# A hybrid decoder step: order of requests and updates around the state stage, and row weights made during routing

## The reference, cut to what matters

```python
# attention (prompt: causal softmax over 256 keys; samples: over 2048 cached keys and their own)
pr = softmax(scores * SCALE);  o_attn = (pr @ v) @ w_o_attn
# state-space branch, prompt, two chunks of 128 tokens, 16 heads in 2 groups
seg = a_cum[:, :, :, None] - a_cum[:, :, None, :]
y_diag = einsum((C B^T) * exp(seg), xdt)              # inside a chunk
chunk_states = einsum(B, exp(a_cum[-1] - a_cum), xdt)
h_final = chunk_decay * h + chunk_states              # h after chunk one is used by chunk two
y_off = einsum(C, h_prev, exp(a_cum))
# state-space branch, samples
h = h * exp(a_t) + outer(x_t * dt_t, b_t);  y = h . c_t      # h is [16, 64, 128] per sample
# gate, norm and output projection, then the mix of the branches
y = rms_norm((y + d_skip * x) * silu(z), g_ssd);  o_ssd = y @ w_o_ssd
merged = sigmoid(gate_a) * o_attn + sigmoid(gate_b) * o_ssd;  x = x + g1 * rms_norm(merged @ w_out)
# experts: sigmoid scores, 4 of 8 groups, 6 of 64 experts, weights normalised to 2.5
w = take(scores, e_idx);  w = w / sum(w) * 2.5
routed = sum_e (silu(t @ w_gate_e) * (t @ w_up_e) * w[:, e]) @ w_down_e
y = x + g2 * rms_norm(routed + shared)
```

## Time and profile before

| what | us |
|---|---|
| median of 3 runs (947.97 to 951.63) | 948.81 |
| the profiled execution | 949.16 |
| its span, first to last instruction | 947.1 |
| PE busy in it | 897.6 (95%) |
| DVE, ACT, POOL busy | 329.3, 201.5, 154.1 |
| bytes read and written, MB | 326.65 and 15.81 |

### The profile page before, as it was taken

One profiled execution on the slowest core, in us unless ns is written; L12 is line 12 of the kernel. 1 busy time (PEld: TensorE's weight loads), 2 busy tenths in 40 slices (PEclk: granted clock), 3 DMA queues, 4 the chain that ended last, 5 costly groups with the idle time before them and its releaser, 6 DMA issues.

```text
span 947.1 us, 18258 instructions
## 1 busy us (share of the span) xinstructions
PE 897.6 (95%) x7475; PEld 556.5 (59%) x7475; DVE 329.3 (35%) x826; ACT 201.5 (21%) x506; POOL 154.1 (16%) x185
## 2 busy tenths in 40 slices
PE   5999999998899799898899999999999999999996
PEld 3888888876565477656744445544454545455442
DVE  2325570056344588346223221221122222221224
ACT  2000110326132398033111111110111111111102
POOL 0000000041565000000212212121212212122110
PEclk9999999999999999999999999999999999999998
DMA  9966757645699819997899999999999999999992
GB/s 367 406 227 232 303 211 291 242 146 202 221 349 348 348 56 316 409 421 295 310 413 400 425 415 426 415 422 419 424 416 424 418 422 419 423 418 423 418 402 107
DMA packets 61237, 325.47 MB, mean 344 GB/s; under 512 B 16321, under 2 KB 25394, under 8 KB 40610
## 3 DMA queue, kind: packets, MB, share of 16 engines
q1 hardware_dynamic: 47250, 305.54, 80.3%
q0 software_dynamic: 12176, 18.56, 5.8%
q10 hardware_dynamic: 1728, 0.18, 0.1%
HBM read 326.65 MB, written 15.81 MB: 362 GB/s over the span
## 4 chain that ended last, share of the span: by engine, by line
PE 45%; DMA 5%; DVE 1%; issue 0%; POOL 0%; ACT 0%
PE bank L2354 22%; PE bank L2294 12%; PE bank L2305 6%; DMA slot_b<-in_w_e 4%; PE bank L2266 3%; DMA xg<-tok_rows,tab_g 1%; PE bank L2388 1%; PE bank L2340 1%; DVE slot_b L2685 0%; DVE slot_b L2693 0%; POOL weight_tab L2214 0%; PE bank L2324 0%; PE bank L2332 0%; ACT slot_b L2498 0%; DVE wgt L2538 0%
## 5 line engine op out<-in xcount | busy, mean ns | idle before, releaser
L420 PE MATMUL bank<-h,ring 128*128 128x264 f32 x608 | 138.4, 388 | 0.5 <-PE bank L420 0.3
L420 PEld LDWEIGHTS bank<-h,ring 128*128 128x128 f32 x608 | 114.6, 190 | 21.9 <-issue 2.8
L2481 ACT ACTIVATE sge<-bank 64x256 f32<-64x256 f32 x64 | 24.1, 377 | 390.6 <-PE bank L2354 390.6
L2584 DVE TENSOR_TENSOR hh<-sge,bank 64x256 f32<-64x256 f32 x64 | 27.1, 423 | 219.0 <-ACT sge L2481 215.5
L2354 PE MATMUL bank<-done_out,xt 128*64 128x256 f32 x832 | 95.5, 382 | 0.0
L2354 PE MATMUL bank<-ring,xt 128*64 128x256 f32 x800 | 91.8, 382 | 0.3 <-ACT xt L2472 0.3
L1668 POOL DMA_INDIRECT xg<-tok_rows,tab_g x32 | 32.0, 1002 | 332.3 <-PE bank L2266 310.6
L2524 DVE COPY sq<-bank 128x512 f32<-128x512 f32 x64 | 44.3, 692 | 104.3 <-PE bank L2294 92.3
L2294 PE MATMUL bank<-ring,ht 128*32 128x512 f32 x320 | 76.4, 598 | 0.0
L2354 PEld LDWEIGHTS bank<-done_out,xt 128*64 128x64 f32 x832 | 57.9, 137 | 27.6
L2305 PE MATMUL bank<-sq,wmat 64*128 64x512 f32 x256 | 72.0, 640 | 0.0
(11 more groups left out here) (486 smaller groups left out, 1245.8 us busy)
## 6 DMA issues: line engine op xcount, KB each, us to landing
done_out<-in_w_e SPq DMA_DIRECT2D x26, 2048.0 KB
ring<-in_w_units SPq DMA_DIRECT2D x25, 2048.0 KB, 10.6
ring<-in_w_e SPq DMA_DIRECT2D x24, 2048.0 KB
slot_b<-in_w_e SPq DMA_DIRECT2D x13, 2048.0 KB
ring<-in_w_e SPq DMA_DIRECT2D x19, 1024.0 KB
slot_b<-in_w_e SPq DMA_DIRECT2D x10, 1024.0 KB
done_out<-in_w_e SPq DMA_DIRECT2D x10, 1024.0 KB
row_of<-in_w_e SPq DMA_DIRECT2D x10, 1024.0 KB
```

The source lines that it names most:

```text
L420: mm = pe.matmul(bank[:, t % NB, 0:T], w[:, j, k, :], h[:, k, :], start=(k == 0), stop=(k == KD - 1))
L2481: act.activation(sg[e % 2][:, :], bank[0:LB, 4, 0:FE], ACT.Silu).then_inc(sg_ready, 1)
L2584: dve.tensor_tensor(hh[e % 2][:, :], sg[e % 2][:, :], bank[LB:2 * LB, 4, 0:FE], ALU.mult).then_inc(hh_ready, 1)
```

## The change: what it does

Seven edits. (1) In prompt attention ACT makes one dummy exponential before `off_part(0)`; PE waits for `max_ready1` 1 ahead of the products of L769 and for 2 only ahead of the transposes behind them; DVE runs `normalise(0)` ahead of the `val` copy. (2) SP no longer requests unit U_OA before `ac`; the request of L929 now brings both U_OA and U_OS, behind `ac` and the states of samples 6 and 7. (3) `h_ready6` also counts the copy of h1, so that `prompt_out(g)` and `states(1)` wait for h1 of their group alone. `final_state(1)` runs behind the samples' part, and `take_out(0)` runs in it, behind its h1 copy. (4) PE runs `prompt_norm(1)` before `attn_part(5)`. (5) The last states are updated in another order: 0 and 1 before `mix(0)`, 2 and 3 behind it, 4 and 5 behind `mix(1)` and `mix(2)`, 6 and 7 inside `mix(3)` between its two products. (6) DVE makes the row weights in the routing block, between its two `hs` products, and POOL stores them there; in the experts' block POOL starts with `gather(2)`, then waits for these stores, gathers the first weights, and issues `gather(3)` behind them. (7) ACT issues two of the four y_s stores.

```diff
@@ prompt attention, ACT, PE, DVE
+                            act.activation(sm[:, 0, 0:1], eps, ACT.Exp)
                             off_part(0)
...
-                            pe.wait_ge(max_ready1, 2)
+                            pe.wait_ge(max_ready1, 1)
...
                             mm.then_inc(lat_done, 1)
+                            pe.wait_ge(max_ready1, 2)
...
+                            normalise(0)
                             dve.wait_ge(v_done, 1)
                             dve.tensor_copy(val[:, :, :], bank[:, 6:8, :]).then_inc(side_took, 1)
-                            normalise(0)
@@ sample attention, SP
-                            sp.wait_ge(weighed, 7)
-                            load_units(sp, U_OA + 1)
@@ state stage, SP and PE
-                        sp.wait_ge(h_ready6, 2)
+                        sp.wait_ge(h_ready6, 4)
...
                             if g:
-                                pe.wait_ge(h_ready6, 1)
+                                pe.wait_ge(h_ready6, 2)
...
-                            pe.wait_ge(h_ready6, g + 1)
+                            pe.wait_ge(h_ready6, 2 * g + 1)
...
                             pe.wait_ge(squares_ready, 5 + g)
-                            pe.wait_ge(h_ready6, 2)
+                            pe.wait_ge(h_ready6, 4)
...
                         attn_part(4)
+                        prompt_norm(1)
                         attn_part(5)
-                        prompt_norm(1)
@@ state stage, DVE
-                            link(dve.tensor_copy(h1[:, hs, :], got[0]))
+                            dve.tensor_copy(h1[:, hs, :], got[0]).then_inc(h_ready6, 1)
+                            dve.wait_ge(h_ready6, 2 * g + 1)
+                            if g:
+                                take_out(0)
...
                         weigh_out(1)
-                        final_state(1)
...
-                        take_out(0)
+                        final_state(1)
...
-                        def mix(d):
+                        def mix(d, between=()):
...
+                            for b in between:
+                                update_state(b)
...
-                        for b in range(3):
+                        for b in range(2):
                             update_state(b)
                         mix(0)
-                        update_state(3)
+                        for b in (2, 3):
+                            update_state(b)
                         for d in range(1, KD):
-                            mix(d)
-                            if d + 3 < TS:
+                            mix(d, (TS - 2, TS - 1) if d == 3 else ())
+                            if d < 3:
                                 update_state(d + 3)
@@ routing block, POOL and DVE; weights() itself is moved here
+                        pool.wait_ge(wgt_ready, 1)
+                        for a, n, lo in ((0, P, 0), (2, P, P), (1, TS, TP)):
+                            pool.dma_start(weight_tab[...], wgt[0:n, a, :]).then_inc(tab_stored, 16)
...
                             dve.tensor_tensor(hs[:, i, :], sg[:, i, :], bank[:, 2 + i, 0:T], ALU.mult)
+                            if i == 0:
+                                weights()
@@ experts' block, POOL
-                        pool.wait_ge(wgt_ready, 1)
-                        for a, n, lo in ((0, P, 0), (2, P, P), (1, TS, TP)):
-                            pool.dma_start(weight_tab[...], wgt[0:n, a, :]).then_inc(tab_stored, 16)
                         gather(pool, AHEAD)
-                        gather(pool, AHEAD + 1)
                         pool.wait_ge(tab_stored, 48)
                         gather_weights(0)
                         gather_weights(1)
+                        gather(pool, AHEAD + 1)
@@ tail, SP and ACT
-                        for c in range(4):
+                        for c in (0, 1):
                             store(sp, io["y"][TP:T, c * QD:(c + 1) * QD], y_s[32 * c:32 * c + TS, :])
+                        act.wait_ge(y_done, 3)
+                        for c in (2, 3):
+                            store(act, io["y"][TP:T, c * QD:(c + 1) * QD], y_s[32 * c:32 * c + TS, :])
```

More of the change, by code:

```diff
@@ L1611, in build @@
             tok_i, tok_j = sb("tok_i", [P, NE // 2], I32, stack=moe), sb("tok_j", [P, NE // 2], I32, stack=moe)
+            wgt, need = sb("wgt", [P, NT, NE], stack=moe), sb("need", [P, NT], stack=moe)
+            tab_w, wv = tok_i, tok_j[:, :].bitcast(F32)
             tok_f = sb("tok_f", [P, NE // 2], stack=moe)
@@ L1636, in build @@
             x_in = [sem(f"xg_in{i}", moe) for i in range(AHEAD)]
+            wgt_ready, tab_stored = sem("wgt_ready", moe), sem("tab_stored", moe)
             xt_done, sgu_done, rows_stored = sem("xt_done", moe), sem("sgu_done", moe), sem("rows_stored", moe)
@@ L1756, in _ @@
                             gather(pool, e)
+                        pool.wait_ge(wgt_ready, 1)
+                        for a, n, lo in ((0, P, 0), (2, P, P), (1, TS, TP)):
+                            pool.dma_start(weight_tab[lo * NE:(lo + n) * NE, :].rearrange("(t e) o -> t (e o)", e=NE),
+                                           wgt[0:n, a, :]).then_inc(tab_stored, 16)
                     @block.tensor
@@ L2064, in _, with weights @@
                         link(dve.tensor_tensor(tab_s[:, :], tab_s[:, :], tok_i[0:LB, :], ALU.add))
+                        def weights():
+                            valid = ccol("valid")
+                            place_f = listed_f[:, 0:NE // 2]
+                            dve.memset(wv, 0.0)
+                            link(dve.tensor_scalar(place_f, tok_f[:, :], float(NE), ccol("second"), ALU.mult, ALU.add))
+                            link(dve.scalar_tensor_tensor(tab_w[:, :], ccol("count")[:, 0:NE // 2], 2.0, place_f, ALU.mult, ALU.add))
+                            link(dve.tensor_tensor(wgt[:, :, :], chosen[:, :, :], score[:, :, :], ALU.mult))
+                            link(dve.tensor_reduce(need[:, :], wgt[:, :, :], AX.X, ALU.add))
+                            link(dve.tensor_tensor(need[:, :], need[:, :], valid, ALU.subtract))
+                            link(dve.tensor_scalar(need[:, :], need[:, :], 1.0, None, ALU.add))
+                            link(dve.reciprocal(need[:, :], need[:, :]))
+                            for a in range(NT):
+                                ins = dve.tensor_scalar(wgt[:, a, :], wgt[:, a, :], need[:, a:a + 1], ROUTE, ALU.mult, ALU.mult)
+                            ins.then_inc(wgt_ready, 1)
                         for i in range(2):
@@ L2078, in build @@
                 yo = [flat_sq[:, i * D:(i + 1) * D] for i in range(NYO)]
-                wgt = sb("wgt", [P, NT, NE], stack=ph)
                 e2 = sb("e2", [TS, NE], stack=ph)
-                need = sb("need", [P, NT], stack=ph)
                 cnt = sb("cnt", [1, NE], stack=ph)
@@ L2113, in build @@
                 tok2 = slot_b[:, 5 * (NBLK - NE):6 * (NBLK - NE)]
-                tab_w, wv = tok_i, tok_j[:, :].bitcast(F32)
                 more_f = slot_b[:, 6 * (NBLK - NE):6 * (NBLK - NE) + (ROUNDS - 1) * HB].rearrange("p (r b) -> p r b", b=HB)
@@ L2128, in build @@
                 ht_done, ht_ready, y_ready = sem("ht_done", ph), sem("ht_ready", ph), sem("y_ready", ph)
-                comb_done, wgt_ready, w_ready = sem("comb_done", ph), sem("wgt_ready", ph), sem("w_ready", ph)
+                comb_done, w_ready = sem("comb_done", ph), sem("w_ready", ph)
                 wv_in = [sem(f"wv_in{i}", ph) for i in range(2)]
@@ L2524, in half_out @@
                             dve.tensor_copy(yo[q % NYO][:, h * 512:(h + 1) * 512], bank[:, b, :]).then_inc(y_ready, 1)
-                        def weights():
-                            valid = ccol("valid")
-                            place_f = wmat[0][:, 0:NPAIR]
-                            dve.memset(wv, 0.0)
-                            link(dve.tensor_scalar(place_f, tok_f[:, :], float(NE), ccol("second"), ALU.mult, ALU.add))
-                            link(dve.scalar_tensor_tensor(tab_w[:, :], ccol("count")[:, 0:NPAIR], 2.0, place_f, ALU.mult, ALU.add))
-                            link(dve.tensor_tensor(wgt[:, :, :], chosen[:, :, :], score[:, :, :], ALU.mult))
-                            link(dve.tensor_reduce(need[:, :], wgt[:, :, :], AX.X, ALU.add))
-                            link(dve.tensor_tensor(need[:, :], need[:, :], valid, ALU.subtract))
-                            link(dve.tensor_scalar(need[:, :], need[:, :], 1.0, None, ALU.add))
-                            link(dve.reciprocal(need[:, :], need[:, :]))
-                            for a in range(NT):
-                                ins = dve.tensor_scalar(wgt[:, a, :], wgt[:, a, :], need[:, a:a + 1], ROUTE, ALU.mult, ALU.mult)
-                            ins.then_inc(wgt_ready, 1)
-                            dve.wait_ge(wgt_ready, 1)
                         def weight_of(k):
@@ L2577, in spread_out @@
```

(1 more changed line is left out.)

6 lines of the change are left out of this document (2 added, 4 removed).

## The result

The changed kernel takes 944.38 us in the median of 21 runs (942.18 to 950.22), the kernel before 949.69 us of 21 (946.5 to 953.4). The ratio is 0.9937 with a 95% interval of 0.9925 to 0.995: 0.6% faster, some 6 us (4.7 to 7.1); the medians alone lie 5.3 us apart. The forecast was 943.6 and a gain of 5.2 us. The profiled execution took 944.14 us, its span 942.0 in place of 947.1. Twelve experiments follow, because the sum came out for partly wrong reasons.

A forecast was written before the change was run, and what follows sets the result against it. The stream of experts' weights was taken as the bound, so time saved before it counts. Terms 0.4 + 3.2 + 0.6 + 0.7 + 0.1 + 0.2 = 5.2 us gave 943.6 us from the median 948.81; range 941.3 to 947.8.

The forecast's parts named there:

- What bounds the kernel: Experts' block: the gapless weight stream ends last, so time saved before it counts, PE time saved inside it does not.
- The growing latencies: Experts' block: weight requests needed 19.8 us at 607.75 and 33.4 us at 876.56, read as a growing backlog.
- The prediction's own sign of being wrong: PE's wait for weights near 910 us stays at 1.0 us, not 2.5, while the block gets shorter.
- the gather's term of 0.1: Row weights from routing: PE's 1.56 us wait for gather(2) goes, but only 0.1 us reaches the end; bounds 0 and 1.6.
- The first rival: PE, not the stream, bounds the experts' block; the gather's 1.56 us count in full, 942.1 us; chance 0.15.
- Prompt attention: Table load moved into ACT's idle time, so exponentials start earlier; gain 0.4 us, bounds 0 and 0.9.
- the larger gain: Prompt attention: a drain of about 1.38 us behind the table load would add up to 1.38 us; not counted.
- The state stage with w_out: State stage to the first w_out matmul: that matmul at 392.6, 4.5 us earlier than 397.08.
- the queue's order and h1: State stage: ac ahead of U_OA and h1 counted by itself start the second halves 3.2 us earlier; bounds 2.2 and 4.3.
- the updates: Last states: one fewer update ahead of mix(0) gives 0.6 us; earlier last store and w_out give 0.7 more.
- What I called 0.7 "more": Behind the state stage: w_out lands at about 390, gaining 0.7 us beyond the 3.8; bounds -2.0 and 1.0.
- Tail: Kernel's end: two of SP's six stores go to ACT in parallel; gain 0.2 us, bounds 0 and 0.7.

The follow-up runs named there:

- e1_early: d1_stores_act with the 32 gate and up matmuls of expert 2 done twice (3.67 us more of PE); 946.09 us, ratio 0.9937.
- e2_late: d1_stores_act with the 32 gate and up matmuls of expert 30 done twice, in the middle of the block; 944.54 us, ratio 0.994.
- after_again: The changed kernel run and profiled once more, with no further edit; 944.31 us, ratio 0.9938.
- d1_stores_act: The changed kernel with the three stores of weight_tab issued by ACT in place of POOL; 943.04 us, ratio 0.9934.
- a5_route: The kernel before with the row weights made and stored in the routing block, alone; 950.2 us, ratio 0.9994.
- b1_no_queue: The changed kernel with the old queue order, U_OA ahead of ac again; 946.59 us, ratio 0.995.
- a3: The kernel before with h_ready6 on h1, final_state(1) and take_out(0) moved and prompt_norm(1) earlier, with the old queue order; 949.68 us, ratio 0.999.
- a4_updates: The kernel before with the new order of the last states' updates, alone; 947.25 us, ratio 0.9974.

## Why the prediction was right, and where it wasn't

- **What bounds the kernel** was wrong in one step: "the stream of weights, which flows without a gap from the block's start". For the first 50 us or so it follows PE (e1_early, and the bytes left), in the middle of the block it does not (e2_late), and at expert 61 PE is only 1 to 2 us ahead. The growing latencies were real, but they grow later. The prediction's own sign of being wrong, a wait of 1.0 us with a shorter block, came in after_again (0.9 us, 1.8 us shorter). So the gather's term of 0.1 was mis-sized: it is 1.7 us where the clock stays full (after_again, d1_stores_act), and nothing where it falls, as in the changed profile, a5_route and b1_no_queue. The first rival, with its 1.56 us, was nearer for this term.
- **Prompt attention**: 0.4 forecast, 0.43 measured at the probabilities of the second half; at those of the first half it was 0.9, as the chain through DVE has it. The table load now stands at 215.57 and lasts 1.28 us, the dummy follows at 216.87. The Trainium skill's drain behind a load (ScalarE: Activation LUTs, What ACT_TABLE_LOAD costs) isn't seen there either, and the trace decides against the larger gain.
- **The state stage with w_out**: 4.5 forecast, 3.8 between the two profiles, 3.4 between the means (77.24 and 73.83), so too large by 1.1: the kernel before's profile, from which I worked, was 0.9 above the mean of the three, and 3.2 us for the queue's order and h1 was the term mis-sized. The forecast times came true almost one by one (L1355 idle 0.4, norm 349.25 for 349.3, `ssd_part(0, 0)` 357.14 for 357.8, second halves 360.8 for 361.5), but that was luck: the stage began 1.8 us earlier, of which the attention edit makes 0.4 and no edit the rest. Counted from the stage's start `ssd_part(0, 0)` came 1.4 us earlier than in before, where I had 2.5, and by the means of the same three and six profiles 0.8; PE ended the stage 2.4 us earlier, where I had 3.8; and its wait behind it is 1.0 us shorter.
- **A loss in the state stage that I didn't have**: PE runs at clock 0.5 for some 4 us, from a point between 339 and 347 us on, in six of the eight profiles with the state stage's edits (not in a3 and e1), and in none of the six without them. There L1355 to `ssd_part(0, 0)` takes 19.9 us, in e1_early 19.1 and in before 18.6; the forecast had 19.4. A window of the changed kernel, where before has clock 1.00:

```profile
340.00:342.00 2.00, 2.00 (x4) 0.88 (x3) 1.94 (x2) 2.00 (x10) 0.00 (x0) 0.50 0.74 285
```

Why it comes there is open; PE's wait at L1355 just before it was 0.4 us in the changed kernel, and 0.75 in e1_early, where the clock stayed full.
- **How it divides** was wrong: I gave 3.2 to the queue's order and h1, and 1.3 to the updates. Alone, the updates give 2.3 us. The others give 0.7 and 0.2, no more than the 1.5 us by which the three profiles without any such edit differ: w_out's landing ends the stage as long as the last store is late. What I called 0.7 "more" is the condition of the rest. The new order of the queue was sized rightly at its landing (2.9 us forecast, 2.4 to 3.0 from issue to landing) and was lost to a slow PE in the profiles with 10 us of clock 0.5 there. The dummy exponential, `prompt_norm(1)` and edit 7 were never run by themselves.
- **Not in the sum at all**: the slow clock behind w_out's wait. It costs 1.68 us, was there in four of five profiles with a late w_out, and with the updates' order it was in none of eight: some 1.3 us on average, if four of five is the rule. And on the other side POOL's stores, which I gave no cost because "DMA idle time" lay beside them: 0.6 us of barrier, and with it, in three profiles of four, the slow clock at the block's start.
- **Tail**: 0.2 forecast. From the last expert's first matmul to the end it is 24.9 us in six profiles without the edit and 24.1 in all seven with it, so 0.8; but a4_updates, without it, had 24.12 as well, so that the edit made it is not shown; part or all of it may be how fast the last stores land. My upper bound of 0.7 us counted only the issuing.
- **Together**: 0.4 + 3.4 + 1.3 - 0.6 + 0.8, and for the gather 1.7 less three times in four 1.69, 0.4: an estimate of 5.7 us from these rows, against 6 measured by the ratio and 5.3 by the medians. The forecast of 5.2 was near by luck as much as by its mechanism: an overestimate (state stage) and an extra cost (barrier) were met by gains that it did not have.

Which kernel is best: d1_stores_act, by 1.3 us of median over after_again. The intervals overlap; what is sure is the 0.6 us of its routing stage, the same in e1_early and e2_late (62.33 to 62.35, for 62.88 to 62.96).

## What to carry to other kernels

When several parts meet at one late transfer, the order of work that issues this transfer can be worth more than all the idle time in front of it, as it was here; look for it first, and don't add the parts up from the front. Take stretches apart over several profiles before sizing a gain of half a per cent: an untouched stretch here scattered by 5.6 us. A stream that is late at the end may well still follow the engine at its beginning; look at the backlog in the first tenth of it.

## What the runs showed of the hardware that I had not expected

A wait of PE can cost twice. Behind waits of 1.7 to 3.2 us PE often ran at a granted clock of 0.5 for about 3 us, which made that work 1.68 or 1.69 us longer, about as much as the shorter of these waits. And three small stores issued by POOL held the end of a block by 0.6 us: the next block's first matmul came 0.70 us behind the landing of the last one in four profiles of four, 3.6 us after its issue in the changed kernel. Issued by ACT they did not hold it.
